# A mixture-of-experts block on one core: first expert's rows by one-hot products, the overflow list made later by GpSimd

## The reference, cut to what matters

```
h = layernorm(concat[meta, x])                       # 528 rows
h = layernorm(ALPHA*h + mixer(h))
logits = h @ w_router + b_router
top_val, top_idx = top_k(logits, 4); gates = softmax(top_val)
order = argsort(top_idx.flatten())                   # rows sorted by expert
xs  = h[order // 4]
hgu = ragged_dot(xs, w_gate_up, sizes) + b_gate_up
out = (ragged_dot(swiglu(hgu), w_down, sizes) + b_down) * gates
h = layernorm(ALPHA*h + segment_sum(out))
```

## Time and profile before

| | |
|---|---|
| median of the runs | 2314.82 us |
| the profiled execution | 2317.71 us, its span 2315.9 us |
| busy PE / DVE / ACT / POOL | 2234.2 / 1668.0 / 1220.7 / 332.9 us |
| TensorE busy, 300 to 400 us | 71.79 us, mean granted clock 0.78 |
| TensorE busy, 400 to 500 us | 98.89 us, clock 1.00 |

### The profile page before, as it was taken

One profiled execution on the slowest core, in us unless ns is written; L12 is line 12 of the kernel. 1 busy time (PEld: TensorE's weight loads), 2 busy tenths in 40 slices (PEclk: granted clock), 3 DMA queues, 4 the chain that ended last, 5 costly groups with the idle time before them and its releaser, 6 DMA issues.

```text
span 2315.9 us, 29232 instructions
## 1 busy us (share of the span) xinstructions
PE 2234.2 (96%) x10480; PEld 1824.7 (79%) x10480; DVE 1668.0 (72%) x1618; ACT 1220.7 (53%) x1229; POOL 332.9 (14%) x274
## 2 busy tenths in 40 slices
PE   7999959999999999999999999889999999999998
PEld 4668847888888888888888888778777778888886
DVE  3646678999999999999999999782557535433434
ACT  2135336767767777677677677643435532322320
POOL 5042011111211111121112111100130010000000
PEclk9999969999999999999999999999999999999999
DMA  7020149999999999999999999862221232222220
GB/s 275 1 85 22 49 148 352 399 394 378 391 386 376 391 377 377 398 377 385 386 381 391 381 375 398 296 238 80 83 86 37 110 119 99 77 105 109 76 107 37
DMA packets 141524, 551.96 MB, mean 238 GB/s; under 512 B 11552, under 2 KB 12704, under 8 KB 124368
## 3 DMA queue, kind: packets, MB, share of 16 engines
q1 hardware_dynamic: 128240, 507.29, 56.8%
q0 software_dynamic: 10736, 38.93, 6.5%
q10 hardware_dynamic: 2480, 4.80, 0.6%
HBM read 523.18 MB, written 25.69 MB: 237 GB/s over the span
## 4 chain that ended last, share of the span: by engine, by line
PE 76%; DVE 5%; issue 1%; DMA 1%; ACT 1%; SPq 0%; DVEq 0%; POOL 0%; ACTq 0%
PE PS L389 73%; PE PS L698 1%; PE PS L692 1%; DVE low L2024 1%; DMA ring<-w_gate_up 1%; ACT act L1726 1%; DVE ring_parts L2311 1%; DVE small L2398 1%; DVE act L1843 0%; DVE st L1816 0%; PE PS L971 0%; DVE act L1848 0%; DMA act<-h_d,tl_c 0%; DVE act L2425 0%; DVE act L2415 0%
## 5 line engine op out<-in xcount | busy, mean ns | idle before, releaser
L389 PE MATMUL PS<-act_parts 128*128 128x512 f32 x3404 | 1072.1, 394 | 17.5 <-DVE act_parts L2179 8.1
L2024 DVE TENSOR_TENSOR low<-ring,act_parts 128x2048 fp32r<-128x2048 f32 x380 | 851.0, 2292 | 34.3 <-ACT act_parts L1486 34.3
L389 PEld LDWEIGHTS PS<-act_parts 128*128 128x128 f32 x3404 | 640.5, 189 | 150.6 <-issue 17.8
L1486 ACT ACTIVATE act_parts<-ring 128x2048 fp32r<-128x2048 f32 x384 | 707.5, 1913 | 16.3 <-issue 5.7
L389 PE MATMUL PS<-low,act_parts 128*128 128x512 f32 x1584 | 618.3, 390 | 0.0
L389 PE MATMUL PS<-act_parts,ring_parts 128*128 128x512 f32 (+1 forms) x1344 | 397.7, 383 | 0.0
L389 PEld LDWEIGHTS PS<-low,act_parts 128*128 128x128 f32 x1584 | 298.2, 188 | 60.4
L389 PEld LDWEIGHTS PS<-act_parts,ring_parts 128*128 128x128 f32 x1344 | 248.3, 188 | 59.0 <-issue 10.7
L389 PE MATMUL PS<-ring_parts,act_parts 128*128 128x512 f32 x1088 | 264.0, 395 | 3.1 <-DVE act_parts L2475 2.1
L389 PE MATMUL PS<-ring_parts 128*128 128x512 f32 (+1 forms) x672 | 255.6, 380 | 0.0
L389 PEld LDWEIGHTS PS<-ring_parts,act_parts 128*128 128x128 f32 x1088 | 206.4, 191 | 49.5 <-issue 3.5
(11 more groups left out here) (263 smaller groups left out, 1715.0 us busy)
## 6 DMA issues: line engine op xcount, KB each, us to landing
ring<-w_gate_up SPq DMA_DIRECT2D x264, 1024.0 KB, 8.9
ring<-w_down SPq DMA_DIRECT2D x132, 1024.0 KB, 8.0
ring<-w_ff SPq DMA_DIRECT2D x16, 2048.0 KB, 7.7
ring<-w_in SPq DMA_DIRECT2D x12, 2048.0 KB, 8.2
ring<-w_o SPq DMA_DIRECT2D x1, 4096.0 KB, 25.0
ring<-w_out SPq DMA_DIRECT2D x2, 2048.0 KB, 7.8
acc_d<-ring POOLq DMA_DIRECT2D x5, 512.0 KB, 3.3
act<-x SPq DMA_DIRECT2D x4, 512.0 KB, 5.7
```

The costliest lines, as they stand in the source:

```text
L389: return eng.matmul(o, lhsT, rhs, start=first, stop=last, **kw)
L1486: A_(W1hi[c % CS], W1[c], ACT.Copy).then_inc(sem["high"], 1)
L2024: tt(W1lo[c], W1[c], W1hi[c % CS].bitcast(F32), ALU.subtract).then_inc(sem["low"], 1)
```

## The change

**Embedding.** The four token tiles are turned first and the meta rows after the first block of products. The last tile is centred by DVE. The first products wait for each feature alone.

**Routing.** `ranks` runs per tile in a bank of its own. DVE makes from it the one-hot of expert 0's slots (`first_hot`), and TensorE makes the turned rows of the first item directly, as 32 products of h with these one-hots (`first_rows`): no list, no gather, no turning. The main list has 31 columns only, in one float32 part: the slot is the plain rank, so no positions are needed, and its 16 products are 64 columns wide. Everything for ranks of 128 and more (`count_past`, `pick`, `over_table`) is computed by GpSimd during items 0 and 1, and TensorE's 16 list products for it stand inside item 1's gate/up product. The bias's and down bias's low parts and the gates' sums and split go to GpSimd as well, and ACT makes the gates' high parts. Base products move behind chunks 4 to 7 of item 0. SP's wait for `acc_d` moves behind expert 1's eighth chunk. `OH`, `listing`, `xs` and others get places of their own.

```diff
 # TensorE
+            def first_rows(t):
+                eng.wait_ge(*past("first_hot", 2 * t + 2))
+                rows = H1[:, t, :].rearrange("s (p k) -> s k p", k=KD)
+                for k in range(KD):
+                    b = 6 + k // 4
+                    if t == 0 and k % 4 == 0:
+                        eng.wait_ge(*free[b])
+                    ins = mm(PS[:, b, k % 4 * P:(k % 4 + 1) * P], rows[:, k, :], OH0[:, t, :], t == 0 and k % 4 == 0,
+                             t == NT - 1 and k % 4 == 3, skip_group_check=True)
+                return ins
+            first_rows(0)
+            first_rows(1)
             ranks(3)
+            first_rows(2)
+            first_rows(3).then_inc(sem["rows_turned"], 1)
...
+            def list_over(t):
+                if t == 0:
+                    take(4, "over_listed", 3)
+                eng.wait_ge(*past("over_made", t + 1))
+                for j in range(TOPK):
+                    ins = mm(PS[:, 4, 0:2 * OVER], over_hot[:, j, :], over_tok[:, j, :], t + j == 0,
+                             t + j == NT + TOPK - 2)
+                ins.then_inc(put("over_psum", 4), 1)
...
+            def first_gate_up():
...
+                for c in range(8):
+                    eng.wait_ge(sem["low"], count_high(0, c))
...
+                    if c == 0:
+                        prefixes()
+                    if c == 3:
+                        turn_gates()
+                    if c >= 4:
+                        base(2 * c - 8)
+                        base(2 * c - 7)
...
             def gate_up(i, over=False):
...
+                        if over and c == 0:
+                            extras_of()
+                        if over and c % 2 == 0:
+                            list_over(c // 2)
 # SP
             for c in range(8):
-                if c == 4:
-                    eng.wait_ge(*past("sums_begun", 80))
-                    load_chunk(0, 10)
-                    load_chunk(0, 11)
                 eng.wait_ge(sem["gate_up_used"], 8 + (c - 7))
                 load_chunk(1, c)
+            eng.wait_ge(*past("sums_begun", 80))
+            load_chunk(0, 10)
+            load_chunk(0, 11)
 # DVE
+                if n == 4:
+                    ts(HN[:, t, :], HN[:, t, :], mv[:, t, 0:1], rst[:, t:t + 1], ALU.subtract, ALU.mult).then_inc(
+                        signal("ln0_last"), 1)
...
+            def first_hot(t):
+                eng.wait_ge(*past("rank_psum", t + 1))
+                eng.tensor_copy(R2[:, t, :], bank_of("rank_psum", t + 1)[:, 0:E]).then_inc(
+                    signal("first_hot"), 1)
+                eng.wait_ge(*latest("first_hot"))
+                ts(OH0[:, t, :], iotas, R2[:, t, 0:1], Mm[:, t, 0:1], ALU.is_equal, ALU.mult).then_inc(
+                    signal("first_hot"), 1)
...
             for t in range(NT):
+                tt(OHs[:, TOPK * t:TOPK * (t + 1), :], iotas.rearrange("p (o e) -> p o e", o=1).to_broadcast([P, TOPK, P]),
+                   spread(rankp[:, TOPK * t:TOPK * (t + 1)], P), ALU.is_equal).then_inc(signal("list_hot"), 1)
+                tt(listing[:, TOPK * t:TOPK * (t + 1), E:2 * E], OH[:, TOPK * t:TOPK * (t + 1), :],
+                   spread(gate[:, t, :], E), ALU.mult).then_inc(signal("list_hot"), 1)
 # GpSimd
+            for hh in range(2):
+                cols = slice(hh * D, (hh + 1) * D)
+                eng.wait_ge(*past("bias_hi", hh + 1))
...
+                tt(bias2[0:E, cols], bgu[0:E, cols], bias2[0:E, cols].bitcast(F32), ALU.subtract).then_inc(
+                    signal("bias_lo"), 1)
...
+            def pick(x, to):
+                for t in range(NT):
+                    chosen = slice(TOPK * t, TOPK * (t + 1))
+                    tt(picked[:, chosen, :], OH[:, chosen, :], x[:, t:t + 1, :].to_broadcast([P, TOPK, E]),
+                       ALU.mult).then_inc(signal("pool_step"), 1)
+                eng.wait_ge(*latest("pool_step"))
+                n = E // 2
+                while n > 1:
+                    tt(picked[:, :, 0:n], picked[:, :, 0:n], picked[:, :, n:2 * n], ALU.add).then_inc(
+                        signal("pool_step"), 1)
+                    eng.wait_ge(*latest("pool_step"))
+                    n //= 2
...
+            def over_table(t):
+                if t:
+                    eng.wait_ge(*past("over_psum", t))
+                for k in range(TOPK):
+                    n = TOPK * t + k
+                    ts(over_hot[:, k, :], iotas, slotf[:, n:n + 1], None, ALU.is_equal).then_inc(signal("pool_step"), 1)
+                    ts(over_tok[:, k, 0:OVER], iotas[:, LAST:ITEMS + 1], itemf[:, n:n + 1], TOKID1[:, t:t + 1],
+                       ALU.is_equal, ALU.mult).then_inc(signal("pool_step"), 1)
+                    ins = ts(over_tok[:, k, OVER:], iotas[:, LAST:ITEMS + 1], itemf[:, n:n + 1], gate[:, t, k:k + 1],
+                             ALU.is_equal, ALU.mult)
...
+            gather(1)
+            by_pick = listing.rearrange("p (t k) c -> p t k c", k=TOPK)[:, :, :, E:2 * E]
...
+            tt(Gf, by_pick[:, :, 0, :], by_pick[:, :, 1, :], ALU.add).then_inc(signal("pool_step"), 1)
...
+            count_past()
+            pick(beyond, itemf)
...
-            next_rows(0)
+            next_select(0)
+            pick(more_past, slotf)
+            over_table(0)
             for t in range(NT):
                 eng.wait_ge(*past("based", 2 * t + 2))
                 eng.dma_start(acc_d[t * P:(t + 1) * P, :], H1[:, t, :]).then_inc(signal("sums_begun", 16), 16)
             eng.dma_start(acc_d[S:S + T, :], H1[:, 0, :]).then_inc(signal("sums_begun", 16), 16)
-            next_select(0)
-            item(1, second=True)
+            next_rows(1)
+            for t in range(1, NT):
+                over_table(t)
+            next_select(1)
```

More of the change, by code:

```diff
@@ L722, in base, with bias @@
                     eng.wait_ge(*past("bd_low", 1))
[L723 to L725 removed]
+                b = 4 + n % 2
+                take(b, "based", n + 1)
                 mm(PS[:, b, :], GT[:, t, :], bd3[:, hf * 512:(hf + 1) * 512]).then_inc(put("base_psum", b), 1)
[L728 to L731 removed]
+            def bias(hh, first):
+                for n in range(2):
+                    cols = slice((2 * hh + n) * 512, (2 * hh + n + 1) * 512)
+                    ins = mm(PS[:, 2 * hh + n, :], sel, bias2[:, cols], first, not first)
+                return ins
@@ L800, in last_down @@
                            hh == 0 and j == 0, hh == 1 and j == 3, place_last(kind, c), **kw)
-            gate_up(0, again=False)
+            first_gate_up()
             turn_gated(0, 0)
             turn_gated(0, 1)
-            with eng.Fori(1, LAST) as i:
+            gate_up(1, over=True)
+            for b in (4, 5):
+                eng.wait_ge(*free[b])
+            down(1)
+            with eng.Fori(2, LAST) as i:
                 gate_up(i)
@@ L1501, in _, with gate_exp @@
             eng.wait_ge(*past("mix_psum", 16))
-            for c in range(1, CS):
-                chunk_high(0, c, first=True)
-            for t in range(NT):
+            def gate_exp(t):
                 eng.wait_ge(*past("tile_routed", 3 * t + 2))
@@ L1526, in _ @@
             rows_high(0)
+            for c in range(4, CS):
+                chunk_high(0, c, first=True)
             def sigmoid(i, hh, again=True):
@@ L2242, in item @@
+            rows_low(0)
+            eng.wait_ge(*past("list_psum", 1))
+            ts(tl_i[:, 0:LAST], bank_of("list_psum", 1)[:, 0:LAST], -1.0, 0.0, ALU.add, ALU.max).then_inc(
+                signal("tokens_listed"), 1)
+            for c in range(1, 4):
+                chunk_low(0, c)
+            list_items()
+            def item(i, second=False):
+                if not second:
+                    chunk_low(i, 0)
                 chunk_low(i, 1)
@@ L2251, in item @@
                     chunk_low(i, c)
+                if second:
+                    list_over()
                 swiglu(i, 1)
                 rows_low(i + 1)
-            for n in range(4):
-                base(n)
-            for c in range(2, 8):
+            for c in range(4, 6):
                 chunk_low(0, c)
             swiglu(0, 0, again=False)
-            for n in range(4, 2 * NT):
-                base(n)
+            chunk_low(0, 6)
+            base(0)
+            base(1)
+            chunk_low(0, 7)
+            for n in range(2, 6):
+                base(n)
+            eng.wait_ge(*past("lam_exp", 1))
+            tt(lamn, small[:, 45:46], small[:, 44:45], ALU.subtract).then_inc(signal("dve_step"), 1)
+            eng.wait_ge(*latest("dve_step"))
+            ts(lamn, lamn, -LAM_INIT, None, ALU.add).then_inc(signal("dve_step"), 1)
+            eng.wait_ge(*latest("dve_step"))
+            chunk_low(1, 0)
+            base(6)
+            base(7)
             swiglu(0, 1, again=False)
             rows_low(1)
-            with eng.Fori(1, LAST) as i:
+            item(1, second=True)
```

(1 more changed line is left out.)

529 lines of the change are left out of this document (266 added, 263 removed).

## The result

The changed kernel takes 2340.75 us (median of 4, 2338.44 to 2340.79) against 2314.43 for the kernel before in the same runs: a ratio of 1.0109, 95% interval 1.0097 to 1.0121. The profiled execution took 2340.74 us with a span of 2338.9. The prediction was 2337, slower, by TensorE's wait for GpSimd in item 1; both hold. Executions of one kernel differ by up to 6 us (the kernel before over 23 runs: 2312.52 to 2318.67), and what stands behind the start of item 2 took 1897.7 to 1902.9 us in the profiled ones.

The account below looks back on a forecast made before the run. TensorE's products were taken as the bound (73% of the span). Span 2315.9 - 3.2 (embedding) + 25.8 (through item 1) = 2338.5; with 1.8 around it 2340.3; median 2.9 under: 2337. Own range 2324 to 2350; 8 in 10: 2296 to 2350.

Parts of the forecast that it names:

- Embedding: Start of the kernel: products start feature by feature at 16.9, 3.7 less, meta turns cost 0.5: -3.2, bounds -1 to -5.
- First-row products: Expert 0's 32 TensorE products from 311.0: eight at low clock, 24 at high, with four ranks, done at 322.1.
- DVE's lists blocked by the two bias parts: Routing, before expert 0's first product: GpSimd's two low parts of the bias block DVE's list one-hots, +4.9.
- First product: Expert 0's first gate/up product stands at 331.0, 15.3 earlier than 346.29; bounds 326 to 337.
- Item 0: Expert 0: work 25.4, waits for gates +2 and base products +3, tail 5.1, selector 1 +2.5; item 1 starts at 369.
- First table: GpSimd's first overflow table: 29 us own work plus 12 subtractions of 2.2, there at 386.5; TensorE wants it at 372.
- one instruction each: Where DVE has two-input and GpSimd any work queued, they alternate on the shared port; a chunk subtraction is 2.2 apart.
- The four waits: TensorE waiting for GpSimd's overflow tables in item 1: 14.5, +6, none at the third, +7, together 27.5.
- The clock after the waits: Item 1: work restarting at the lower clock level after TensorE's stalls costs 2 us.
- Rival 1: Overflow tables: DVE's subtractions seldom hold GpSimd, item 1 starts at 359 and costs +4.0 - 1.6; 2298, chance 0.28.
- rival 2: Overflow tables: GpSimd slips two or three operations between subtractions, or they cost half; stalls near 6; 2316, chance 0.12.
- Rival 3: First rows: main case, but the clock stays low through them as from 310 to 315; +6, 2343, chance 0.10.

Follow-up runs that it names:

- experiment 1: Kernel before with only the embedding part of the change (reordered turns, products waiting per feature): 2310.75 us, ratio 0.9981.
- experiment 3: Changed kernel with first-row products reading 128 neighbouring features as stationary operand instead of every eighth: 2339.30 us.
- experiment 6: Changed kernel with neighbouring features as stationary operand, and GpSimd's first-bias work started after tile 2's one-hot instead of tile 3's: 2333.54 us, ratio 1.0080.
- experiment 11: experiment 10 with another feature order (128 features per group of eight) in gate/up weight loads, first-row products and turned rows: 2306.07 us, ratio 0.9965.
- experiment 10: experiment 9 with GpSimd's low parts of the first bias started after tile 2's one-hot instead of tile 3's: 2311.23 us, ratio 0.9984.
- experiment 4: Changed kernel with the same tables in fewer, longer GpSimd instructions (pick products fused, 6 instead of 12 instructions a table): 2331.95 us, ratio 1.0075.
- experiment 5: Changed kernel with each of DVE's 2048-element subtractions of items 0 and 1 split into two of 1024: 2337.44 us, ratio 1.0099.
- experiment 2: Changed kernel without rows past each expert's first 128: picks and most counting left out, tables zero, list products kept: 2305.03 us, ratio 0.9956.
- experiment 9: Changed kernel with overflow tables made by DVE, GpSimd's pick products fused, list products behind chunks 1, 3, 5, 7 of item 1: 2311.27 us, ratio 0.9986.
- experiment 7: Changed kernel with overflow lists one item later (item 2, behind chunks 1, 3, 5, 7) and two table buffers: 2328.20 us, ratio 1.0061.

## Why the prediction was right, step by step

**Embedding: direction right, size too small by 1.5 to 2.8.** Predicted -3.2 with a bound of -5; it moved by 6.0 in the profiled execution and by 4.65 in experiment 1. The start of the products, 16.9 predicted, was 16.87 in experiment 1 and 15.56 in the changed kernel's profiled execution: I priced the turns at 0.2 each from the earlier trace rows, and the 32 took 6.57 there and 5.25 here. The meta turns behind the first block took 0.66, where I had 0.5. What the sum lacks in both is the clock behind the 2.47 of waiting that goes away: in the kernel before it was 0.50 from 20.9 to 24.3 us, with the first products in it, and in experiment 1 it was 1.00 from 16 to 22.

**First-row products: 11.1 predicted, 16.3 measured** (305.3 to 321.6, with the ranks of tile 3). This step failed in size. I gave every product the price of its clock, 0.128 or 0.256 an instruction; they took 0.246 at either. The weight loads over 300 to 325 us (group by form: busy, mean ns), after and in experiment 3:

```profile
L394 PEld LDWEIGHTS PS<-act,ring 128*128 128x128 f32 x64 | 15.4, 336 | 0.0
```

```profile
L394 PEld LDWEIGHTS PS<-act,ring 128*128 128x128 f32 x64 | 10.1, 252 | 0.0
```

The same 64 loads cost 5.3 less when they read neighbours, and experiments 6 and 11, where DVE's lists are earlier too, turn that into time at the first product.

**DVE's lists blocked by the two bias parts: +4.9 predicted, 4.3 measured.** One one-hot took 2.83 instead of 0.68, one product 2.45 instead of 0.28. In the changed kernel this did not decide, as TensorE's strided products ended with it (experiment 10); without the stride it did (3 against 6).

**First product.** 331.0 predicted, 327.8 with the embedding's share, and 325.55 measured: 2.3 earlier, 2.8 of it the embedding's. The products' 5 us too many hardly showed. Only the half ahead of tile 3's ranks holds DVE: they stood 8.7 after the start of the first rows where I had 7.3, and DVE's lists took 9.9 from there where I had 11.3. The two chains then ended together, DVE's low rows at 325.1 and TensorE's list products at 325.6.

**Item 0: 38.0 predicted from first product to item 1, 36.6 measured** (325.55 to 362.15), with the waits that were named: 1.2 for the gates (2 predicted), 1.7 for a base product (3), 4.2 for DVE's tail (3.1 before). The 2.5 for selector 1 did not come; TensorE never waited for it.

**First table.** Predicted: 29 us of GpSimd's own and 12 blocks of 2.2, 55.5 from the first product, with 14 subtractions possible. Measured: 381.95 - 325.55 = 56.4, with 14 subtractions in the stretch. The split was right too: 13 instructions of GpSimd were held (one of them twice), and what they took above their free values adds up to 26.0, which leaves 30.4. That is less than the 33.2 of the 14 subtractions: on average 1.9 were lost to each, not its whole 2.3. GpSimd's instructions averaged 0.98 (50.10 over 51), as I had named for a sign, and one-input steps of 128 elements took 0.54 to 0.64 where nothing held them, two-input ones 0.45 to 0.46: it was right to go by the row for them. The words "one instruction each" carry less than I rested on them: here the subtractions that DVE still has to do decide, not how many instructions GpSimd brings (experiments 4 and 5). As the forecast counted DVE's, its number came out.

**The four waits: 14.5, 6, 0, 7 predicted; 15.0, 2.6, 0, 7.0 measured.** GpSimd needed for the second table just the 12.5 predicted (381.95 to 394.4). But TensorE's work between the two lists took 9.7 (382.1 to 391.9) instead of 6.3, at the lower clock, so it waited 3.4 less: part of the clock's cost hid in the wait.

**The clock after the waits: +2 predicted, some 6 to 8 measured** (30.4 of experiment 2 less 24.6, or 8.0 within item 1). This term was mis-sized. TensorE's rows at 382 and 416 show 0.50 for five microseconds each.

**Sum.** Predicted -3.2 + 25.8 = 22.6 on the profiled execution, measured 23.1: embedding -2.8, first product +0.5, item 0 -1.4, item 1 +4.2 (74.0 against 69.8: 2.9 less of waits, the clock 4 to 6 more). So the total is nearer than its parts, which is luck: the parts off by 1.4 to 4.2 cancel. From the sum for the profiled execution, 2340.3 against 2340.74, I took 2.9 to get at the median; the changed kernel's median was that of its profiled execution, and this is most of the 3.7 between 2337 and 2340.75. Rival 1 (GpSimd keeps up, 2298) and rival 2 (half the cost, 2316) are excluded by the 24.6 of waits. Rival 3 is excluded: the granted clock was 0.98 from 310 to 315 and 1.00 over the second half of the first rows (313.82 to 321.61), which took long for another reason.

The gain was there too. In experiment 2 the first product is 19.9 earlier than before (326.35 against the earlier trace rows's 346.29), item 2 only 7.3. Of the difference item 0 took 9.1 (37.98 against 28.83): prefix, gate and base products, ahead of the first product before, now stand behind it, and two waits came with them; item 1 took 3.5, where the list products now stand. So even without any wait for tables the main list on its own was worth 2.6 us there beside the embedding's 4.65.

## What to carry to other kernels

Work moved to an idle engine must be priced with what the engine's neighbour does in the same stretch. Where DVE and GpSimd both have queued work, count the instructions of both. In these runs, where DVE's queue ran dry now and then, GpSimd's chain lasted its own time plus most of DVE's (30 and 26 of 33 us); where it never did, GpSimd got about one instruction per DVE instruction, and a deadline 38 us later took only 7 of the 24.6 us of waiting away. The same tables cost DVE 1.4 us each; made by GpSimd they cost TensorE 24.6 us of waiting.

A wait of the bound engine can cost more than its length (24.6 cost 30 to 33 here), and a gain that is covered by the next engine in line needs both removed before it shows (stride and bias parts).

A change of several parts should be compared with its best part alone. Measured against the kernel before, experiment 9 looks like a small win; measured against the embedding part alone, its routing part wins nothing.

## What the runs showed of the hardware

- f32 products whose stationary operand is read with a stride of 8 elements took 0.246 us an instruction at a granted clock of 0.68 and of 1.00; read contiguously 0.12 at 1.00. The turns of an item read with the same stride took 1.04 for 8 instructions (experiment 10, at 432.79), contiguous ones 1.03 (experiment 11, at 461.30), so turning does not pay it.
- 28 GpSimd instructions ran beside 27 of DVE in 44 us in which DVE was busy 43.4 and GpSimd waited for TensorE for 3.8; with DVE's subtractions halved, 33 beside 42, with 8.1 of such waiting.
- GpSimd's indirect DMA issue is held too: 2.25 at 329.10 beside a DVE subtraction, 1.05 at 385.74 without one.
- One GpSimd instruction of 128 elements took 4.65 us, two subtractions long, and one of 17 elements 6.62 (experiment 7); why they lost several turns running no run here shows.
